# Strassen products for a transformer MLP: the down projection's three quarters in seven products instead of eight

## The reference

```python
def sq_relu_mlp(h, w1, w2):                      # w1: 1024 x 4096, w2: 4096 x 1024
    return jnp.square(jax.nn.relu(h @ w1)) @ w2

for l in range(DEPTH):                           # DEPTH = 2
    need_ctx = l < DEPTH - 1                     # the first layer works on the context too
    ...
    x = x + g2 * sq_relu_mlp(h, w_mlp1[l], w_mlp2[l])
    if need_ctx:
        ...
        xc = xc + g2c * sq_relu_mlp(hc, w_mlp1[l], w_mlp2[l])
```

## Time and profile before

| | |
|---|---|
| median of 3 runs | 3364.2 us (3360.8 to 3364.57) |
| span of the profiled execution | 3361.6 us |
| PE, PEld busy | 99%, 82% |
| DVE, ACT, POOL busy | 49%, 36%, 54% |
| DMA | 358.56 MB, mean 107 GB/s |
| first layer's MLP in the second block | about 2084 to 2640 us from the start |

### The profile page before, as it was taken

How to read it: one execution, slowest core, us unless ns; L and a number is a source line. 1 busy time by engine, 2 the same in 40 slices (tenths; PEclk the granted TensorE clock), 3 DMA queues, 4 the chain that set the end, 5 groups by cost and what they waited for, 6 DMA issues and landing times.

```text
span 3361.6 us, 49896 instructions
## 1 busy us (share of the span) xinstructions
PE 3318.0 (99%) x17394; PEld 2747.4 (82%) x17394; DVE 1644.2 (49%) x2565; ACT 1223.8 (36%) x1991; POOL 1799.5 (54%) x2004
## 2 busy tenths in 40 slices
PE   8999999999999999999999999999999999999999
PEld 6778888888767888888888878888888788788887
DVE  4543257788544238778856445211212664442113
ACT  4433342224434233323434553221212435543223
POOL 5325568887434558888465223433434464246555
PEclk9999999999999999999999999999999999999999
DMA  5213345454322335555353112222211442133333
GB/s 173 82 51 95 99 139 180 168 179 135 112 66 66 97 96 192 169 176 176 108 135 92 50 54 91 70 63 63 62 63 63 120 126 76 57 113 107 96 98 107
DMA packets 106428, 358.56 MB, mean 107 GB/s; under 512 B 12000, under 2 KB 22496, under 8 KB 104352
## 3 DMA queue, kind: packets, MB, share of 16 engines
q1 hardware_dynamic: 71712, 257.13, 24.1%
q10 hardware_dynamic: 34560, 99.30, 9.2%
HBM read 336.79 MB, written 8.59 MB: 103 GB/s over the span
## 4 chain that ended last, share of the span: by engine, by line
PE 92%; issue 4%; DVE 2%; POOL 1%; ACT 1%; DMA 0%; ACTq 0%; POOLq 0%; DVEq 0%
PE ps L1028 9%; PE ps L1029 9%; PE ps L1030 9%; PE ps L683 8%; PE ps L685 8%; PE ps L684 8%; PE ps L937 3%; PE ps L939 3%; PE ps L938 3%; PE ps L1136 3%; PE ps L1137 3%; PE ps L1138 3%; PE ps L707 2%; PE ps L708 2%; PE ps L709 2%
## 5 line engine op out<-in xcount | busy, mean ns | idle before, releaser
L589 POOL TENSOR_TENSOR w_lo<-w_raw,w_hi 128x256 fp32r<-128x256 f32 x1904 | 1692.0, 921 | 1518.9 <-ACT w_hi L1505 1505.2
L1505 ACT ACTIVATE w_hi<-w_raw 128x1024 fp32r<-128x1024 f32 x472 | 498.7, 1057 | 730.6 <-PE ps L1030 328.8
L683 PE MATMUL ps<-h_hi,w_hi 128*128 128x512 f32 x944 | 373.3, 395 | 0.0
L685 PE MATMUL ps<-h_hi,w_lo 128*128 128x512 f32 x944 | 368.6, 391 | 0.0
L684 PE MATMUL ps<-h_lo,w_hi 128*128 128x512 f32 x944 | 368.6, 390 | 0.0
L2371 DVE SCALAR_TENSOR_TENSOR ada_junk<-ada_w,c_silu 128x1024 f32<-128x1024 f32 x192 | 320.2, 1668 | 3.3
L1136 PE MATMUL ps<-c_hi,w_hi 128*128 128x512 f32 (+1 forms) x832 | 298.4, 359 | 5.6 <-DVE vm L2630 3.2
L1137 PE MATMUL ps<-c_lo,w_hi 128*128 128x512 f32 (+1 forms) x832 | 285.9, 344 | 0.0
L1138 PE MATMUL ps<-c_hi,w_lo 128*128 128x512 f32 (+1 forms) x832 | 285.7, 343 | 0.0
L1028 PE MATMUL ps<-c_hi,w_hi 128*128 128x512 f32 (+1 forms) x792 | 279.1, 352 | 3.1 <-DVE c_lo L2542 3.1
L1029 PE MATMUL ps<-c_lo,w_hi 128*128 128x512 f32 (+1 forms) x792 | 278.3, 351 | 0.0
(11 more groups left out here) (384 smaller groups left out, 6141.3 us busy)
## 6 DMA issues: line engine op xcount, KB each, us to landing
w_raw<-in_w SPq DMA_DIRECT2D x476, 512.0 KB, 3.6
ada_w<-in_ada ACTq DMA_DIRECT2D x96, 512.0 KB, 3.6
zs<-stage ACTq DMA_DIRECT2D x52, 128.0 KB, 2.1
m_row<-m_spill ACTq DMA_DIRECT2D x16, 384.0 KB, 5.4
wq_row<-wq_spill ACTq DMA_DIRECT2D x16, 384.0 KB, 5.4
x_spill<-x ACTq DMA_DIRECT2D x2, 2048.0 KB, 6.9
zs_m<-zm ACTq DMA_DIRECT2D x32, 128.0 KB, 2.1
bias<-in_rpb ACTq DMA_DIRECT2D x8, 512.0 KB, 3.5
```

The costliest lines, as they stand in the source:

```text
L589: last = nc.gpsimd.tensor_tensor(w_lo[:, j, c], w_raw[:, j % RAW, c], w_hi[:, j, c].bitcast(F), ALU.subtract)
L683: nc.tensor.matmul(bank, w_hi[:, j, w], rhs_hi[:, k, :], start=(k == 0), stop=False)
L685: last = nc.tensor.matmul(bank, w_lo[:, j, w], rhs_hi[:, k, :], start=False, stop=(k == n - 1))
L1505: nc.scalar.activation(w_hi[:, j, :], w_raw[:, j % RAW, :], ACT.Copy).then_inc(hi_ready, 1)
```

## The change

In the first layer of the second block, the down products of the first three quarters (3072 hidden features) are made by Strassen's scheme in Winograd's form: a product of 2 x 2 blocks in seven block products instead of eight. The three quarters become six blocks of 512 hidden features. A block's four tiles of hidden features are two pairs `e`; a pair gives the 2 x 2 of token blocks: two tiles by two halves of the 768 tokens (384 each: `b11, b12` of the even tile, `b21, b22` of the odd). A down chunk now holds 512 features by 256 outputs, four quarters `a11, a12, a21, a22` of 256 columns, one half for each `e`.

- **Order of the stream**: one up chunk, then per block 4 up chunks and 4 down chunks, so that the last of a block's up chunks belongs to the next block; the last quarter as before. The number of chunks stays.
- **Weights**: DVE makes three sums of quarters in `s_raw` and one in place in `w_raw` (`part_sums_of`, 4 operations of 256 columns), ACT rounds `s_raw` to `s_hi` (768 columns) and the chunk to `w_hi`, POOL makes `s_lo` (3 subtractions) and `w_lo` (4). `s_raw` is free for the next when POOL has made `s_lo`.
- **Tokens**: relu and square go to `hid` (two halves of 768 columns, by turns). Per pair DVE makes four sums of 384 columns (`token_sums_of`), ACT rounds to `t_hi` in two copies (4 x 384 and 3 x 384 columns), DVE subtracts for `t_lo` in two. ACT's relu of the next pair waits for the last `t_lo`, as it writes over `hid`.
- **PE**: 7 products for a down chunk, each 2 x 3 matmuls of 384 columns, in three banks: `run` is never cleared within the chunk but goes on accumulating, and DVE adds it to the stream at four points. PE waits for `seventh_read` ahead of the third, fourth, fifth and seventh product.
- **DVE** makes 7 additions of 384 columns to the stream for a chunk, three of them in two operations (256 of context, 128 of `x`); in down chunk 0 also the square of the up chunk ahead.
- Semaphores of the neighbourhood attention (`ns_ready`, ...) are replaced by those of the first block's attention, with other counts; no instruction is added.

```diff
+    def mlp_by_sevens(up, down):
+        tile(up, 0)
+        for b in range(HALF_BLOCKS):
+            for t in range(1, BLOCK_FF + 1):
+                tile(up, (b * BLOCK_FF + t) * P)
+            rows = [np.concatenate([np.arange(t * P, (t + 1) * P) for t in (b * BLOCK_FF + e, b * BLOCK_FF + e + 2)]) for e in range(2)]
+            for m in range(0, KT, 2):
+                put(*[block(down, rows[e], np.arange(t * P, (t + 1) * P)) for t in (m, m + 1) for e in range(2)])
+        q = QUARTERS - 1
+        for m in range(1, KT):
+            tile(up, q * D_MODEL + m * P)
+        for m in range(KT):
+            put(block(down, q * D_MODEL + every, np.arange(m * P, (m + 1) * P)))
...
+    t_hi = sb("t_hi", DYN, [2, 7, ALL // 2], R)
+    t_lo = sb("t_lo", DYN + 21 * KB, [2, 7, ALL // 2], R)
+    t_sum = sb("t_sum", DYN + 42 * KB, [3, ALL // 2])
+    hid = sb("hid", DYN + 54 * KB, [2 * ALL])
+    s_raw = sb("s_raw", DYN + 49 * KB + 512, [3 * QUAD])
+    s_hi = [sb(f"s_hi{j}", GATE + 3 * KB * j, [3 * QUAD], R) for j in range(RING)]
+    s_lo = [sb(f"s_lo{j}", DYN + at, [3 * QUAD], R) for j, at in enumerate((46 * KB + 512, 63 * KB, 66 * KB, 69 * KB))]
...
+            def lower_parts(g, j, pair):
+                pool.wait_ge(parts_hi, pair + 1)
+                for a in range(0, 3 * QUAD, LOWER):
+                    c = slice(a, a + LOWER)
+                    last = nc.gpsimd.tensor_tensor(s_lo[j][:, c], s_raw[:, c], s_hi[j][:, c].bitcast(F), ALU.subtract)
+                last.then_inc(parts_free, 1)
+                lower(g, j)
...
+            def seventh(bank, j, main, part, quad, wide, fresh, sums):
+                hi, lo = (w_hi[:, j, :], w_lo[:, j, :]) if main else (s_hi[j], s_lo[j])
+                for e in range(2):
+                    if sums:
+                        pe.wait_ge(tokens_lo, sums[e])
+                    w = slice(part * QUAD + e * P, part * QUAD + (e + 1) * P)
+                    t_h, t_l = t_hi[:, e, quad, 0:wide], t_lo[:, e, quad, 0:wide]
+                    nc.tensor.matmul(ps[:, bank, 0:wide], hi[:, w], t_h, start=(fresh and e == 0), stop=False, skip_group_check=True)
+                    nc.tensor.matmul(ps[:, bank, 0:wide], hi[:, w], t_l, start=False, stop=False, skip_group_check=True)
+                    last = nc.tensor.matmul(ps[:, bank, 0:wide], lo[:, w], t_h, start=False, stop=(e == 1), skip_group_check=True)
+                return last
...
+            def down_by_sevens(L, b, g, need_ctx):
+                wide = wide_half(need_ctx)
+                normed(g + 1, 0, need_ctx)
+                for m in range(BLOCK_FF):
+                    at, j = down_at(g, m)
+                    done = pair_of(L, b, m) * 6
+                    sums = [sums_of(L, b, e) * 2 for e in range(2)]
+                    run, second, third = SEVEN_BANKS[m % 2]
+                    arrive(at, j)
+                    if m < 2:
+                        pe.wait_ge(bank_read[m + 2], g + 3)
+                    else:
+                        pe.wait_ge(bank_read[m - 1], g + 4)
+                        pe.wait_ge(seventh_read, pair_of(L, b, m - 1) * 6)
+                    seventh(run, j, True, 0, 0, wide, True, None if m else [n + 1 for n in sums]).then_inc(seventh_ready, 1)
+                    seventh(third, j, True, 2, 4, wide, True, None if m else [n + 2 for n in sums]).then_inc(seventh_ready, 1)
+                    pe.wait_ge(seventh_read, done + 1)
+                    seventh(run, j, False, 1, 5, wide, False, None).then_inc(seventh_ready, 1)
+                    pe.wait_ge(seventh_read, done + 2)
+                    seventh(third, j, False, 2, 3, wide, False, None).then_inc(seventh_ready, 1)
+                    pe.wait_ge(seventh_read, done + 3)
+                    seventh(run, j, False, 0, 1, wide, False, None).then_inc(seventh_ready, 1)
+                    seventh(second, j, True, 1, 2, wide, True, None).then_inc(seventh_ready, 1)
+                    pe.wait_ge(seventh_read, done + 5)
+                    seventh(run, j, True, 3, 6, wide, False, None).then_inc(chunk_used, 1)
...
+            def up_after_sevens(L, b, g, need_ctx):
+                for j in range(1, RING):
+                    if j == 1:
+                        pe.wait_ge(bank_read[3], g + 2)
+                        pe.wait_ge(seventh_read, pair_of(L, b, -1) * 6)
+                    if j == 2:
+                        pe.wait_ge(seventh_read, pair_of(L, b, 0) * 6)
+                    if j == 3:
+                        pe.wait_ge(bank_read[0], g + 3)
+                    normed(g, j, need_ctx)
...
+            def mlp_by_sevens(L, g, need_ctx):
+                down_by_sevens(L, 0, g, need_ctx)
+                with pe.Fori(1, HALF_BLOCKS) as b:
+                    up_after_sevens(L, b, g + b * 2, need_ctx)
+                    down_by_sevens(L, b, g + b * 2, need_ctx)
+                up_after_sevens(L, HALF_BLOCKS, g + 2 * HALF_BLOCKS, need_ctx)
+                for j in range(RING):
+                    normed(g + 2 * HALF_BLOCKS + 1, j, need_ctx)
...
+                def split_parts(g, j, pair):
+                    act.wait_ge(chunk_used, g * RING + (j + 1))
+                    act.wait_ge(part_sums, pair * 4 + 4)
+                    nc.scalar.activation(s_hi[j][:, :], s_raw[:, :], ACT.Copy).then_inc(parts_hi, 1)
+                    nc.scalar.activation(w_hi[:, j, :], w_raw[:, j % RAW, :], ACT.Copy).then_inc(hi_ready, 1)
+                def tokens_upper(L, b, e):
+                    n, wide = sums_of(L, b, e), wide_half(need_ctx)
+                    act.wait_ge(token_sums, n * 4 + 2)
+                    nc.scalar.activation(t_hi[:, e, 0:4, 0:wide], hid[:, 0:4 * wide].rearrange("p (q t) -> p q t", q=4), ACT.Copy).then_inc(tokens_hi, 1)
+                    act.wait_ge(token_sums, n * 4 + 4)
+                    nc.scalar.activation(t_hi[:, e, 4:7, 0:wide], t_sum[:, :, 0:wide], ACT.Copy).then_inc(tokens_hi, 1)
+                def positive(g, j):
+                    at = j % 2 * 2 * wide_half(need_ctx)
+                    act.wait_ge(chunk_used, g * RING + (j + 1))
+                    if need_ctx:
+                        nc.scalar.activation(hid[:, at:at + CTX], ps[:, 4 + j, 0:CTX], ACT.Relu)
+                    nc.scalar.activation(hid[:, at + ALL - SEQ - lo:at + ALL - lo], ps[:, j, :], ACT.Relu).then_inc(bank_read[j], 1)
+                def block_of_sevens(L, b, g):
+                    for j in range(1, RING):
+                        if j == 2:
+                            act.wait_ge(tokens_lo, sums_of(L, b, 1) * 2)
+                        positive(g, j)
+                        split_parts(g, j, pair_of(L, b, j - 1))
+                        if j % 2:
+                            tokens_upper(L, b, j // 2)
+                    act.wait_ge(tokens_lo, sums_of(L, b, 2) * 2)
+                    positive(g + 1, 0)
+                    split_parts(g + 1, 0, pair_of(L, b, RING - 1))
+                    for m in range(BLOCK_FF):
+                        split(*down_at(g, m))
+                def mlp_by_sevens(L, g):
+                    positive(g, 0)
...
+                def part_sums_of(g, j, pair):
+                    a11, a12, a21, a22 = [w_raw[:, j % RAW, a * QUAD:(a + 1) * QUAD] for a in range(4)]
+                    s3, s2, s4 = [s_raw[:, a * QUAD:(a + 1) * QUAD] for a in range(3)]
+                    dve.wait_ge(raw_ready[j % RAW], g * 32 + 16 * (j // RAW + 1))
+                    if not isinstance(pair, int) or pair:
+                        dve.wait_ge(parts_free, pair)
+                    nc.vector.tensor_tensor(s3, a11, a21, ALU.subtract).then_inc(part_sums, 1)
+                    nc.vector.tensor_tensor(a21, a21, a22, ALU.add).then_inc(part_sums, 1)
+                    dve.wait_ge(part_sums, pair * 4 + 1)
+                    nc.vector.tensor_tensor(s2, a22, s3, ALU.subtract).then_inc(part_sums, 1)
+                    dve.wait_ge(part_sums, pair * 4 + 3)
+                    nc.vector.tensor_tensor(s4, a12, s2, ALU.subtract).then_inc(part_sums, 1)
+                def squared(g, j):
+                    one = hid[:, j % 2 * 2 * wide:(j % 2 + 1) * 2 * wide]
+                    dve.wait_ge(bank_read[j], g + 3)
+                    nc.vector.tensor_tensor(one, one, one, ALU.mult).then_inc(v2_ready, 1)
+                def token_sums_of(b, e):
+                    n, done = sums_of(L, b, e), squares_before(L) + 2 * e
+                    b11, b12, b21, b22 = [hid[:, a * wide:(a + 1) * wide] for a in range(4)]
+                    t1, t2, t4 = [t_sum[:, a, 0:wide] for a in range(3)]
+                    dve.wait_ge(v2_ready, b * BLOCK_FF + (done + 1))
+                    nc.vector.tensor_tensor(t1, b12, b11, ALU.subtract).then_inc(token_sums, 1)
+                    dve.wait_ge(v2_ready, b * BLOCK_FF + (done + 2))
+                    nc.vector.tensor_tensor(b12, b22, b12, ALU.subtract).then_inc(token_sums, 1)
+                    dve.wait_ge(token_sums, n * 4 + 1)
```

(42 more changed lines are left out.)

189 lines of the change are left out of this document (136 added, 53 removed).

## The result

The changed kernel takes 3378.9 us (median of 5 runs, 3378.88 to 3380.68) beside 3364.6 for the kernel before (3360.8 to 3366.82), a ratio of 1.0044, 95% interval 1.0032 to 1.0057: slower by some 14.4 us. The forecast was 3370, with 3361 to 3376 for its own mechanism and 3348 to 3386 in all. The profiled execution has a span of 3377.1 us, 15.5 longer than before.

The account below looks back on a forecast made before the run. PE, busy 99% of the span, was taken as the bound. Products -26.7, handshake +2, stalls +13.5 and +9.4, clock +6.8 gave +5.0 on the 3364.2 us median: 3370 us, forecast range 3361 to 3376, overall 3348 to 3386.

Parts of the forecast that it names:

- its own mechanism: DVE's sums ahead of each block's down chunks delay PE and use up the products' gain; likeliest 3370 us, chance 0.45.
- products: Down chunks: 42 matmuls of 384 columns at 0.1735 us replace 48; 201.6 us becomes 174.9, giving back 26.7 us.
- handshake: Within down chunks PE waits for DVE's bank reads; one wait costs about 0.1 us a chunk, 2 us in all.
- stall, five blocks: Down chunk 0 of later blocks: PE waits for the first bank read, 2.7 us a block, 13.5 us in all.
- stall, first block: The first block has no lead on DVE's chain: 6.2, 0.6 and 2.6 us of waits, 9.4 us together.
- clock: Half clock behind the first block's pause and three of the five others, 1.7 us each, 6.8 us.
- rival (a): DVE's chain 0.8 us longer, PE also waits before the first product: 4.4 us a block, 3384 us; chance 0.20.
- Rival (b): POOL mostly idle during DVE's chain, which ends about 3 us sooner: 3348 us, 3342 without contention; chance 0.22.
- (c): Slower handshake in down chunks: a wait costs 0.3 to 0.4 us, 7 us more, 3377 us; chance 0.08.
- (d): Down-chunk matmuls of 384 columns cost what 512 do: some 3420 us; chance 0.05 together with others.
- The rule that speaks against the change: Contended DVE sums would wait POOL's whole 0.70 us, not 0.54: stall near 5.5 us a block, total some 17 us worse.
- The gap rule: Skill's matmul pace, 2.4 GHz plus 2.5 ns: 0.1625 us for 384 columns, gain some 11 us larger; not used.

Follow-up runs that it names:

- tokens_first: `spread` plus down chunk 2's weight sums and their ACT copies moved behind the second pair's token sums and lower parts; 3350.3 us, ratio 0.9959.
- less_pool: Changed kernel with POOL making one of three `s_lo` differences per down chunk, used for all three products (results differ); 3358.9 us.
- late: Changed kernel with DVE making down chunk 3's four weight sums after chunk 0's seven reads, not ahead of them; 3362.9 us.
- spread: Changed kernel with down chunk 3's four weight sums placed one each behind reads 2 to 5 of down chunk 1; 3355.2 us.
- filled: Changed kernel plus matmuls where PE waited: 60 ahead of the first block's first product, 8 or 12 ahead of each block's third; 3371.8 us.
- filled_best: `tokens_first` plus 42 matmuls of 384 columns filling the first block's pause ahead of its first product; 3349.9 us.

## Why the prediction came out as it did

The terms of the sum, beside what the traces show:

| term | forecast | measured | from |
|---|---|---|---|
| products | -26.7 | -26.6 | pace 0.1736 us |
| handshake | +2 | +2 | 6 x 0.33, `tokens_first` |
| stall, five blocks | +13.5 | +16.9 | 5 x 3.37 |
| stall, first block | +9.4 | +14.6 | 16.68 - 2.08 |
| clock | +6.8 | +8.3 | 4 x 1.57, and 2.0 |
| sum | +5.0 | +15.2 | down phases +15.0 |

The sign, the mechanism and its place were right: DVE's weight sums and tokens' sums ahead of the first bank read, not POOL, ACT, the loads or the handshake. The time was nearer to rival (a) than to the forecast. It lay outside 3361 to 3376, which the forecast's own mechanism had, and inside 3348 to 3386 only because that range was widened for rivals, which did not happen. That it fell inside is therefore partly luck. Rival (a) wanted PE to wait for the four quads in every block. They were due at 8.92 and came at 8.7, 0.2 us short of deciding. Its price of 4.4 us a block does not follow from its condition either: a chain 0.8 us longer puts the first bank read, and PE with it, 0.8 us later, which is 3.5. Rival (b) needed POOL out of the way; `less_pool` and `tokens_first` had to bring that about. (c) and (d) fall by the table's first two lines.

**The step that failed is the first block,** 5.2 of the 10 us. The forecast took the ends of the ramp's three chunks from ACT's relus, "at about 2107.5, 2110.2 and 2113.1 (relus at 2107.69 and 2110.44)". But ACT copies weights between two relus and is itself behind, so the second and third relu say when ACT was free, not when PE had finished. PE's own starts tell it (changed kernel, timeline of PE; then ACT's):

```profile
2109.26 0.39 PE L1114 MATMUL ps<-c_hi,w_hi 128*128 128x512 f32 x1
...
2117.64 0.40 PE L1114 MATMUL ps<-c_hi,w_hi 128*128 128x512 f32 x1
```

```profile
2108.10 0.38 ACT L2263 ACTIVATE hid<-ps 128x256 f32<-128x256 f32 x1 [8.95 <-PE ps L1116]
...
2108.85 1.06 ACT L1657 ACTIVATE w_hi<-w_raw 128x1024 fp32r<-128x1024 f32 x1
2109.80 0.39 ACT L2263 ACTIVATE hid<-ps 128x256 f32<-128x256 f32 x1
```

The fourth chunk starts at 2109.26, the chunk ahead at 2117.64, the first product at 2126.04, 8.4 us apart; in the kernel before the ramp ends 0.4 us sooner, at 2108.85. The three chunks' last blocks are three 512-column matmuls each, so they end 0.68 us apart, not 2.75. The third ends 4.25 us before my 2113.1, PE stands at the end of its own work that much sooner, and DVE, whose chain was right within 0.8 us (lower part at 2137.67, less the 0.4 by which the ramp ended later, for 2136.5), is waited for that much longer. The evidence was in the rows: the 512-column matmuls that start at 2093.20 run on at 0.2273, and 72 of them from about 2092.5 end at 2108.9.

**The steady stall** was right in kind and 0.7 us low, 3.4 us of the 10. Its chain started 0.3 us later (-1.5 for -1.8), the four sums from 2200.28 to 2203.88 took 3.6 us for 3.4, the second lower part 1.8 for 1.7: each step was rounded down a little. The remaining 0.11 is the first matmul behind a pause. Errors in steps that all lie on the path add up, and nothing hides them.

**The clock**: four of five fell, three were taken, and 2.0 us in the first block for 1.7. That the last two are near each other is luck: the forecast priced a stretch of 3.41 us, the trace has one of 17.07, of which only the last 4.5 us cost anything. The count of four is a draw as well (see Open). The price per fall, 1.7 us as half of 3.41, was a little high: at half clock a 384-column matmul starts each 0.32 us for 0.1735, so 3.41 us give the work of 3.41 x 0.1735 / 0.32 = 1.85 at full clock and cost 1.56, and the blocks show 1.6.

**The rule that speaks against the change.** Rows 8 had a contended operation wait 0.54 us beside a POOL operation of 0.70. After shows the same at another size: 0.55 us for 384 columns alone (2200.28), 1.10 beside POOL (2200.75), and in `less_pool` three operations are shorter by 0.54 us each when POOL is out of the way. The Trainium skill (SBUF — State Buffer, "Who interferes with whom") has the first comer hold the shared ports "for the whole instruction", which would be 0.70. It says this beside DVE's 2-port modes; of an operation with two SBUF inputs it says that it contends, without a time. The traces agree that DVE is blocked and not slowed in proportion, as 256, 384, 1152 and 1536 columns mostly pay the same 0.54 us. Only the fourth of a row of sums pays less, 0.43 to 0.44 (0.85 for 0.42, 0.99 for 0.55). By 0.70 the four quads' lower part would have passed 8.92, and PE's timeline shows no pause there.

**The gap rule.** The measured pace of 384 columns, 0.1736 us, decides between the halfway point of the rows and the estimate of 0.1625 by the Trainium skill (TensorE: Matmul & The Clock Gate, "Back-to-back issue gap"): the rows were right to 0.0001, the rule 6% low for this kernel's three-for-one matmuls.

**Open**: why one pause of 2.39 us in five drew no half clock. Its length does not decide. A pause of 2.37 us near 1995 us, ahead of this MLP and the same in all eight traces, was followed by half clock before the change and in `late`, `spread`, `filled` and `filled_best`, and not in the changed kernel, `less_pool` and `tokens_first`. In the changed kernel the clock fell at 2683.15, behind a pause of 1.81 us that ended at 2681.61, shorter than the 1.95 that drew none in rows 12. What does decide, no run here shows. At 1.6 us each, such falls outside this MLP can be a part of why medians and down phases differ by up to 1.3 us. And whether the first block's remaining 7.4 us can be had by another order was not tried; the sums of chunk 0 and of the first pair of tokens would have to change places with work that is no less due.

## What to carry to other kernels

Before an engine is given work to spare another, write out its queue at the one place where the other must wait for it, and put first what the waiting engine needs first: the change as made lost 14 us, and the same instructions with eight sums of each block moved behind the tokens' (four of them with their copies) won 14. Take the time at which an engine has finished from that engine's own rows, never from its consumer's, which may be the one that is late. And price a low clock only over the work that nobody else holds up.

## What the runs showed of the hardware beyond what was expected

- Pauses of PE and the granted clock, in these MLPs: 0.87 us (six blocks of `late`) and 1.12 us (five of `less_pool`) drew no half clock, 2.39 to 2.40 us did in four cases of five, 7.38, 9.18 and 11.0 us always (five traces), for 10.24 to 17.07 us. This is no threshold: the 2.37 us near 1995 us drew it in five of eight traces. Matmuls whose result nobody needs kept it at 1.00.
- At half clock matmuls of 384 columns start 0.32 us apart for 0.1735 at full clock, a factor of 1.84 and not 2.
- A DVE operation with two SBUF inputs beside a busy POOL mostly takes 0.54 us more, whatever its own size from 256 to 1536 columns (0.43 to 0.44 more in the fourth of a row of sums), and POOL pays as well. In the changed kernel's second block four splits of POOL, usually 2.83 us, took 5.94:

```profile
2203.43 5.94 POOL L646 TENSOR_TENSOR w_lo<-w_raw,w_hi 128x256 fp32r<-128x256 f32 x4
```
